# Stick-breaking attention turned around: queries on the partitions, suffix sums as reversed scans

## The reference

```python
z = einsum('bhtd,bhsd->bhts', q[lo:hi], k[:hi]) * scale      # t: query, s: key
mask = s < t
log_keep = where(mask, log_sigmoid(-z), 0)
tail = cumsum(log_keep, axis=keys, reverse=True) - log_keep
A = where(mask, exp(log_sigmoid(z) + tail), 0)
out = einsum('bhts,bhsd->bhtd', A, v)
```

## Time and profile before

| | |
|---|---|
| time, median of 3 runs | 1332.89 us (1331.8 to 1333.66) |
| span of the profiled execution, first to last instruction | 1327.0 us |
| time of the profiled execution beside its span | not listed apart from the three times above; the median is 5.9 us above the span |
| PE busy | 1204.8 us, 91% |
| VectorE, ScalarE, GpSimd busy | 556.6, 426.5, 309.7 us |
| DMA | 55.37 MB, 42 GB/s on average |
| first unit of stick-breaking to the last | 484 to 817 us |

### The profile page before, as it was taken

One profiled execution on the slowest core, in us unless ns is written; L12 is line 12 of the kernel. 1 busy time (PEld: TensorE's weight loads), 2 busy tenths in 40 slices (PEclk: granted clock), 3 DMA queues, 4 the chain that ended last, 5 costly groups with the idle time before them and its releaser, 6 DMA issues.

```text
span 1327.0 us, 24240 instructions
## 1 busy us (share of the span) xinstructions
PE 1204.8 (91%) x10200; PEld 912.4 (69%) x10200; DVE 556.6 (42%) x858; ACT 426.5 (32%) x862; POOL 309.7 (23%) x291
## 2 busy tenths in 40 slices
PE   4798999999998998999988997779799899998996
PEld 4476876667686664454764453678699788788996
DVE  4345388774534223333754332664411600154114
ACT  5423001232411135664335564223300611254003
POOL 1241111333211111120220000546744023500220
PEclk9799999999999999999998999879899999999998
DMA  6111000111000000010110001322522012200113
GB/s 193 39 32 25 21 15 26 26 31 40 21 22 18 25 18 17 17 29 4 33 33 1 1 0 48 97 65 81 190 65 80 0 33 64 64 1 1 33 33 127
DMA packets 71723, 55.37 MB, mean 42 GB/s; under 512 B 2944, under 2 KB 67520, under 8 KB 71616
## 3 DMA queue, kind: packets, MB, share of 16 engines
q1 hardware_dynamic: 71616, 53.83, 13.5%
HBM read 49.63 MB, written 4.19 MB: 41 GB/s over the span
## 4 chain that ended last, share of the span: by engine, by line
PE 66%; DVE 14%; ACT 13%; issue 3%; POOL 2%; DMA 1%; DVEq 0%; ACTq 0%; SPq 0%; POOLq 0%
PE bank L843 12%; PE bank L856 10%; PE bank L845 9%; PE bank L844 9%; ACT B L1153 4%; PE bank L1097 4%; PE bank L1099 4%; PE bank L1098 4%; DVE A L1449 3%; ACT A L1153 2%; PE bank L1036 2%; DVE yT L1452 2%; PE bank L1067 2%; PE bank L1047 2%; DVE B L1452 2%
## 5 line engine op out<-in xcount | busy, mean ns | idle before, releaser
L843 PE MATMUL bank<-act_hi,whi 128*128 128x512 f32 (+1 forms) x752 | 319.4, 425 | 10.0 <-POOL wlo L793 8.3
L845 PE MATMUL bank<-act_hi,wlo 128*128 128x512 f32 (+1 forms) x752 | 287.5, 382 | 0.0
L844 PE MATMUL bank<-act_lo,whi 128*128 128x512 f32 (+1 forms) x752 | 287.4, 382 | 0.0
L792 POOL TENSOR_SCALAR whi<-wraw 128x512 fp32r<-128x512 f32 x94 | 71.3, 758 | 708.2 <-PE bank L845 673.6
L843 PEld LDWEIGHTS bank<-act_hi,whi 128*128 128x128 f32 x752 | 145.1, 193 | 70.6 <-issue 34.8
L845 PEld LDWEIGHTS bank<-act_hi,wlo 128*128 128x128 f32 x752 | 145.4, 193 | 29.2
L844 PEld LDWEIGHTS bank<-act_lo,whi 128*128 128x128 f32 x752 | 146.4, 195 | 20.5 <-issue 1.9
L856 PEld LDWEIGHTS bank<-A 64*64 64x64 f32 x3712 | 120.7, 139 | 50.2 <-issue 24.9
L1097 PE MATMUL bank<-vhi,act_hi 128*128 128x256 f32 x512 | 146.2, 286 | 8.3 <-DVE x L1786 3.0
L856 PE MATMUL bank<-A 64*64 64x64 f32 x3712 | 133.1, 225 | 19.9 <-DVE A L1596 13.3
L1098 PE MATMUL bank<-vlo,act_hi 128*128 128x256 f32 x512 | 145.0, 283 | 0.0
(11 more groups left out here) (156 smaller groups left out, 1407.5 us busy)
## 6 DMA issues: line engine op xcount, KB each, us to landing
wraw<-in_w_in SPq DMA_DIRECT2D x62, 256.0 KB, 2.9
A<-in_x SPq DMA_DIRECT2D x8, 512.0 KB, 3.7
vraw<-in_w_out SPq DMA_DIRECT2D x16, 256.0 KB, 2.8
x<-in_x SPq DMA_DIRECT2D x8, 512.0 KB, 7.0
wraw<-in_wq SPq DMA_DIRECT2D x16, 256.0 KB, 2.7
vraw<-in_wo SPq DMA_DIRECT2D x16, 256.0 KB, 2.7
out<-yT SPq DMA_DIRECT2D x8, 512.0 KB, 2.6
B<-in_wk SPq DMA_DIRECT2D x8, 256.0 KB, 2.8
```

The costliest lines, as they stand in the source:

```text
L792: done(pool, nc.gpsimd.tensor_scalar(hi, raw_view[slot], 1.0, 1.0, ALU.mult, ALU.mult), "w_hi")
L843: mm(bank, wh, act_hi[:, k, cols], start=k == 0, stop=False)
L844: mm(bank, wh, act_lo[:, k, cols], start=False, stop=False)
L845: ins = mm(bank, wl, act_hi[:, k, cols], start=False, stop=k == KT - 1)
```

## The change

Queries are now on the partitions and keys in the columns. A unit is one block of 128 queries, up to 512 keys, and both heads of a pair, in a PSUM tile of two banks (`duo`), one bank for each head. There are 24 units of 128, 256, 384 or 512 keys (4, 4, 4 and 12), again 18,432 columns over all heads. `duo` takes the place of both banks before, so there is one such tile and not two.

- `sbz`: z as matmuls of K = 64 with 128 columns each, the two heads in turn (144 matmuls in all). At the diagonal a matmul of the identity with a mask of -1e30 in fp32r comes first for each head (32 matmuls); this replaces the masks on VectorE. Abs, Exp and Ln on ScalarE take both heads in one instruction. VectorE adds max(z, 0), runs one reversed scan for each head (started by the last value of the unit before), and subtracts the sum from z.
- `sbt`: PE turns the 128 x 128 blocks (144 transposes) back into `duo`; Exp on ScalarE for both heads at once, into one buffer where there were two halves.
- `sbv`: 144 matmuls with the values, each with 128 columns and 64 outputs, the two heads in turn.
- `sbo` takes both heads at once. The triangle, the running sums, and two thirds of the HOLD entries are gone; stick-breaking may begin when step 8 of the second RWKV pair is done, where it was held until step 11. Two copies of 128 x 128 are added to `derive`.

```diff
-HOLD = {('sbz', 0, 0, 0, 0): ('cu', 1, 11), ('sbz', 0, 0, 1, 0): ('cu', 0, 9), ... ('sbz', 1, 0, 0, 0): ('cu', 1, 8), ...
+HOLD = {('sbz', 0, 0, 0): ('cu', 1, 8), ('sbz', 1, 0, 0): ('cu', 1, 8), ...
...
+                if u < n:
+                    c = share(u)
+                    step(stick, ("sbz", i, th, u), [("P", 0.9 * c + 0.2), ("AE", 2.8 * c + 0.5), ("D", 5.4 * c + 0.3)])
+                if u:
+                    step(stick, ("sbv", i, th, u - 1), [("P", 0.9 * share(u - 1))])
+                if u < n:
+                    step(stick, ("sbt", i, th, u), [("P", 0.9 * c), ("AE", 0.9 * c + 0.2)])
...
-        sz = Ring("sz", [5, 6])
+        sz = Ring("sz", [duo[:, :, :]])
+        tn = Ring("tn", [duo[:, 0, :], duo[:, 1, :]])
...
 PE, sbz
+                if diag:
+                    for hd in range(2):
+                        mm(bank[:, hd, w - P:w], ident_r[:, :], above_r[:, :], start=True, stop=False)
+                for c in range(w // P - 1, -1, -1):
+                    add = diag and c == w // P - 1
+                    for hd, r in enumerate(heads):
+                        ins = mm(bank[:, hd, c * P:(c + 1) * P], B[r, 0, tb * P:(tb + 1) * P],
+                                 B[r, 1, k0 + c * P:k0 + (c + 1) * P], start=not add, stop=True)
 PE, sbt
-                ins = mm(bank[:, a:a + n], tri, spb[:, a:a + n], start=False, stop=u == 0, skip_group_check=True)
...
-                    ins = mm(bank[:, a:a + n], negone, rsb[:, a:a + n], start=False, stop=True, skip_group_check=True)
+                for hd in range(2):
+                    for c in range(w // P):
+                        ins = tr(bank[:, hd, c * P:(c + 1) * P], e[:, hd, c * P:(c + 1) * P], ident)
 PE, sbv
+                for c in range(w // P - 1, -1, -1):
+                    j = k0 // P + c
+                    for hd, r in enumerate(heads):
+                        ins = mm(bank[r, :], B[:, 2, j * P + hd * HD:j * P + hd * HD + HD], at[:, hd, c * P:(c + 1) * P],
+                                 start=j == tb, stop=j == 0, skip_group_check=True)
 ScalarE, sbz and sbt
+                done(act, av(e, bank[:, :, 0:w], ACT.Abs), "act_step")
+                exp(e, e, scale=-1.0)
+                done(act, av(e, e, ACT.Ln, bias=1.0), "sp_ln")
...
+                sz.rd_done(act, av(two_heads(B[:, 5, :], w), bank[:, :, 0:w], ACT.Exp), key)
 VectorE, sbz
+                stt(sp, bank, 0.0, sp, MAX, ADD)
+                for hd in range(2):
+                    start = 0.0 if sb_diagonal(th, u) else c[:, hd, 0:1]
+                    ok(V.tensor_tensor_scan(c[:, hd, ::-1], one.broadcast_to([P, w]), sp[:, hd, ::-1], start, MUL, ADD))
+                tt(e, bank, c, SUB, "e_ready")
```

More of the change, by code:

```diff
@@ L163, in mixer_chains @@
         step(stick, ("sv", i), [("P", 0.6), ("A", 1.1)], *[proj("s", i, w) for w in "vqk"])
[L164 to L177, removed]
+        for th in range(2):
+            units = sb_units(th)
+            n = len(units)
+            for u in range(n + 1):
+                share = lambda v: units[v][2] / HALF
+                if u < n:
[5 more added lines that the diff above has]
+                    step(stick, ("sbt", i, th, u), [("P", 0.9 * c), ("AE", 0.9 * c + 0.2)])
+            step(stick, ("sbo", i, th), [("D", 0.8)], proj("s", i, "gate"))
     follows = {}
@@ L415, in program @@
         m_incl = fcst[:, 4 * P + CH:4 * P + 2 * CH]
+        one = fcst[:, 4 * P + 2 * CH - 1:4 * P + 2 * CH]
+        ident_r = sb("ident_r", [P, P], F32R)
+        above_r = sb("above_r", [P, P], F32R)
         def lev(l):
@@ L439, in program @@
             vraw = st.enter_context(nc.sbuf_tensor("vraw", [P, 2, 2, 256], F32))
-        banks = [ctx.enter_context(nc.psum_tensor(f"bank{i}", [P, HALF], F32)) for i in range(8)]
+        banks = [ctx.enter_context(nc.psum_tensor(f"bank{i}", [P, HALF], F32)) for i in range(5)]
+        duo = ctx.enter_context(nc.psum_tensor("duo", [P, 2, HALF], F32))
+        last = ctx.enter_context(nc.psum_tensor("bank7", [P, HALF], F32))
+        whole = [b[:, :] for b in banks]
         sems, counts = {}, {}
@@ L473, in bank @@
             def bank(self, key):
-                return banks[self.ids[self.units[key][0]]][:, :]
+                return self.views[self.units[key][0]]
             def ready(self, b):
@@ L570, in program @@
             elif name == "sv":
-                for h in range(2):
-                    sz.plan((name,) + a + (h,))
+                sz.plan((name,) + a)
             elif name == "sbz":
-                p, hd, th, u = a
-                j = sb_blocks(th)[u]
-                sz.plan(("z", p, hd, th, j), reads=2 if j >= 4 * th and sb_cols(th, j)[1] > P else 1, posts=2)
-                if u == 0:
-                    so.plan(("o", p, hd, th))
+                sz.plan(("z",) + a, posts=2)
+                if a[2] == 0:
+                    so.plan(("o",) + a[:2])
             elif name in ("vtr", "wide"):
@@ L624, in wait_av, with two_heads @@
                 return
-            if sb_units[g][3] == 0:
-                so.rd_open(eng, ("o",) + sb_units[g][:3])
-            else:
-                eng.wait_ge(sem("av_done"), sum(u[3] != 0 for u in sb_units[:g + 1]))
+            if sb_last(*sb_order[g]):
+                so.rd_open(eng, ("o",) + sb_order[g][:2])
+            else:
+                eng.wait_ge(sem("av_done"), sum(not sb_last(*v) for v in sb_order[:g + 1]))
+        def two_heads(buf, w):
+            return buf.rearrange("p (e s) -> p e s", e=2)[:, :, 0:w]
         wides = [("o", n) for n in range(4)] + [("f", n) for n in range(4)]
```

236 lines of the change are left out of this document (89 added, 147 removed).

## The result

The changed kernel takes 1352.64 us (median of four runs, 1348.20 to 1353.06), the kernel before 1332.35 us beside it (1327.45 to 1333.66). The ratio is 1.0185, 95% interval 1.0131 to 1.0240: slower by 20 us, where I forecast 1308 and faster.

The account below looks back on a forecast made before the run. TensorE's work and, after 817 us, a chain of small steps set the time. 472 + 147 + 60 + 147 + 96 = 922 against 943, taken as -25: span 1302, plus 5.9, 1308 us; forecast's range 1290 to 1322, all cases 1268 to 1355.

Parts of the forecast that it names:

- the single tile decides against it: Rival: both stick-breaking pairs' chains wait in three in-order queues; at 4 us a unit about 1348 us; chance 0.28.
- TensorE's work: Stick-breaking's own instructions on TensorE fall from 146 to 73 us (55 to 113), with the array's halves overlapping.
- the 14 us for changes between whole and half arrays: Within TensorE's new work: 0.2 us per change, three visits for each of 24 units; 0 if hidden.
- The bare chain: Stick-breaking's units without queue waits: 12.5 us a full unit, 119 us for each pair of heads.
- The waits: In stick-breaking's pairs, waits behind other work in three engines' queues: 2.3 us a unit, making a pair 147 us.
- The projections between: Between stick-breaking's pairs: q, k, v of the second pair with HGRN2's levels, 60 us.
- HGRN2's second pair inside stick-breaking's, 30 of 98 us off the end: Some HGRN2 steps run in TensorE's gaps during stick-breaking's second pair, cutting the mixers' end from 126 to 96 us.
- The start at 470 and not 472: Stick-breaking's first pair was to begin three RWKV steps earlier, at 472 and not 484 us.
- the rounding from 922 to 918: The mixers' end summed to 922 us, -21 against 943; the forecast took -25 for the whole.
- The 5.9 us that I put between span and median: Added to the forecast span of 1302 us to give the forecast time of 1308.
- RWKV's end: The RWKV pair ends some 25 us later, as its steps wait behind stick-breaking's longer blocks on VectorE.
- The two signs: Wrong if full stick-breaking units come further apart than 16 us, or HGRN2's second pair still begins behind stick-breaking.

Follow-up runs that it names:

- The run with the other order: The changed kernel with only the planner's last resort leaning to RWKV and HGRN2, so HGRN2's levels lie among stick-breaking's units; 1378.33 us, ratio 1.0409.
- the joined values: The two-tile kernel with one head per unit, value products issued for both heads together after the second head's Exp; 1326.89 us, ratio 0.9995.
- Idle products: The changed kernel plus up to 24 unused 512-column TensorE products ahead of the transposes of units in the idle stretches; 1344.27 us, ratio 1.0142.

## Why the prediction was wrong

The prediction called the time faster and gave "the single tile decides against it" 0.28 and 1348 us; it came out at 1352.64. That the rival's figure is so near is luck: it wanted 40 us from waits in the two pairs, which gave 13; most of the rest came from the end of the mixers. By its steps, from the end of its sum (918) to the 965 us measured:

- **TensorE's work**, 146 to 73 us: the mechanism held. At full clock the rows give 18 x (1.16 + 1.09 + 1.09) = 60 us and 32 mask products at about 0.17 us, 5 us: 65 us. The halves overlap, and the 14 us for changes between whole and half arrays were not there. They had no ground in the rows either: I set the duration of a half-array product (1.05) against the distance of starts of a whole-array one (0.86), while the duration of that one is 1.02 in the earlier trace rows. The trace shows 41 + 49 = 89 us on B, as part of it ran at the low clock (0.82 and 0.69 on average). "TensorEngine Tiling (Array Packing)", section "Tiling Modes", of the Trainium skill agrees with this row where it says that tiles work in parallel.
- **The bare chain**, 12.5 us a full unit and 119 us a pair: right (12.2 us as read above). Two scans of 512 keys took 2.48 to 2.60 us, as the scan in the earlier trace rows. The groups of the narrowest and the widest scan:

```profile
L1723 DVE TENSOR_TENSOR_SCAN B<-fcst,B 128x512 f32<-128x512 f32 x24 | 30.3, 1264 | 0.8
L1723 DVE TENSOR_TENSOR_SCAN B<-fcst,B 128x128 f32<-128x128 f32 x8 | 3.7, 459 | 0.3
```

  That is 0.805 us for 384 elements, a slope of 2.15 us per 1024, and 0.19 us fixed. The Trainium skill states half throughput for the scan in "DVE: opcode table, instruction layouts, handler registers and perf-mode slots", section "Datapath and trigger behaviour". The trace agrees: the slope is twice the pass's 1.07. In the prediction I set this slope against the whole time of a scan, 2.58 us, and so found a difference that is not there.
- **The waits**, 2.3 us a unit: the second pair took 148 us against 147. But the waits weren't those I named: late in that pair nothing stood in the queues, and about 2 us a full unit were the 1.2 GHz clock. That the length fits within 1 us is luck. The first pair, where other work did stand there and the clock was low from 510 to 570 us, took 159 us, so 3.3 us a unit. Over both pairs it is (307 - 238) / 24 = 2.9 us: 13 us on the sum.
- **The projections between**, 60 us: 68, with TensorE busy for 65.4 of them. HGRN2's first pair had begun 19 us before the end of stick-breaking's first (gate at 610 us), and the stretch was no shorter than before (66). The miss is 8 us; no run takes this stretch apart.
- **HGRN2's second pair inside stick-breaking's, 30 of 98 us off the end**: this step failed, and is the largest term. The end took 120 us and not 96. The gate was early (746 us), the levels were not. The run with the other order showed that the premise was false and not only the planner's choice: beside the single chain, idle TensorE was not room for HGRN2. The 34 us that the end lost came back as 61 us on the second pair. I treated gaps as free time, while they are the places where an in-order queue stands behind a link of the other chain.
- The start at 470 and not 472, the rounding from 922 to 918, and the rest at 385.8 and not 384 make up the remaining 4 us: 13 + 8 + 24 - 2 + 4 + 2 = 49, and 1302 + 49 is the span of 1351. The 5.9 us that I put between span and median were 1.8 here, so the time is 45 us off and not 49.
- **RWKV's end** 25 us later: right (567 us against 541), and of no weight: undoing it gained nothing.

The two signs that I had named stand on either side: two full units on end stayed under 16 us apart, if barely (15.8 us between those of 588.7 and 604.5 us), and HGRN2's gate was ahead of stick-breaking's end, but its levels were not. The sign should have been the levels. And 0.2% is not what a measurement here can tell: the interval of the result is 0.5% to either side.

Behind the sum is one sentence that the prediction had and weighed too little: fewer columns on TensorE don't shorten a unit. Before, two units were open, and TensorE did its work on one while ScalarE and VectorE had the other. The change halved that work, by its full-clock times, and left one unit open. TensorE's idle time, 52.5 us up to the output projection before, is 126 us after (495 us from 470 to 965, less 369 busy in the five windows): the work saved turned into waiting. The prediction allowed for 100 us of idle time (52.5 + 73 - 25). The run with one head per unit and two tiles gives the price of having one unit open, 37 us, and with it the sign; of these, 17 us come back inside the one tile by taking the heads apart.

What is open: how much of the 12 us by which the joined values lost is clock and how much is the wait, and how much of the two-tile gain is the order of stages.

## What to carry to other kernels

Ask first how many units are in flight after the change, not only how much work each has. A saving on the fullest engine that closes a second buffer turns its work into waiting; here two open units of one head were worth 37 us, although z and values cost 39 us more of TensorE. And a gap on an engine with an in-order queue isn't by itself room for another chain of small dependent steps: with one unit open, two such chains run beside each other took 27 us more than in turn. If a forecast relies on such a gap, look for which instruction the queue stands at in it.

## What the runs showed of the hardware

TensorE's granted clock in the second pair fell to 0.69 on average, and to 0.50 (1.2 GHz) from 800 to 845 us, where it was busy for 20 of 45 us (before, at 116 of 127 us, it was 0.97). Eight fp32 transposes of 128 x 128 took 1.97 us there and 1.09 at full clock, and eight products of z 2.08 and 1.16. Idle products raised the average to 0.89. In the second pair they gave back 7 us; in the first they gave 1, as they held up the transposes of one unit by 4.5 us in TensorE's queue.

Products of two heads on the two halves of the rows (or of the columns), issued in turn, overlap in full: 8 in 1.16 (1.09) us, and 4 of one head alone in the same time. A reversed fp32 scan with an fp32 factor costs 2.15 us per 1024 elements and 0.19 us for each instruction, twice the slope of a plain pass; a forward scan of 1024 elements with a byte factor took 2.29 us in the same trace.
